# A hybrid decoder layer on one core: negated row maxima, whole copies of the softmax outputs, and low parts and a state decay moved from VectorE to GpSimd

## The reference, cut to what matters

```
h = rms_norm(x, norm1_w);  y = h @ w_in                      # 1024 -> 3852 columns
fox:       logits = q @ k.T * 64**-0.5 + c_i - c_j (causal), p = softmax(logits), o = p @ v        # 4 heads of 64
retention: o = chunked linear attention with fixed decay; o = head_rms(o) * silu(rg)               # 4 heads of 64
gdn:       per chunk: u = u0 - w @ state;  o = q_g @ state + attn @ u                              # 4 heads of 128
           state = state * exp(g_last) + k_tail.T @ u
           o = head_rms(o) * gdn_norm_w * silu(gz)
x = x + concat(fox, retention, gdn) @ w_out                  # 1024 -> 1024
h = rms_norm(x, norm2_w)
x = x + sum over the two chosen experts of (silu(h @ w1) * (h @ w3) * gate) @ w2     # 32 experts, width 256
out = rms_norm(x, final_norm_w)
```

## Time and profile before

| | us |
|---|---|
| median of 3 runs (620.01 to 622.05) | 621.25 |
| the profiled execution's own time | 619.92 |
| its span, first to last instruction | 618.0 |
| busy: PE | 579.1 (94%) |
| busy: DVE | 245.6 (40%) |
| busy: ACT | 198.6 (32%) |
| busy: POOL | 179.8 (29%) |
| mean granted TensorE clock | 0.995 |

### The profile page before, as it was taken

The page is one execution under the profiler, slowest core; times in us unless marked ns, Lnnn a source line. Parts: engine busy times, 40 slices in busy tenths (PEclk is TensorE's granted clock), DMA queues, the critical chain, the costliest instruction groups (busy, mean ns, idle before and its releaser), DMA issues.

```text
span 618.0 us, 12011 instructions
## 1 busy us (share of the span) xinstructions
PE 579.1 (94%) x4922; PEld 446.4 (72%) x4922; DVE 245.6 (40%) x618; ACT 198.6 (32%) x429; POOL 179.8 (29%) x118
## 2 busy tenths in 40 slices
PE   7999999999999999999899999999999999987892
PEld 5987887799999888856679998666555565654440
DVE  6135553592216711287732146323332233321117
ACT  7344544523324261634635321111111121111113
POOL 1443434173268422421433301111112111120014
PEclk9999999999999999999999999999999999999997
DMA  9665443422121122003788878999999999999975
GB/s 338 202 187 157 146 134 97 134 70 51 56 70 36 37 69 70 1 2 122 271 325 305 318 265 313 357 421 423 428 422 427 423 429 423 423 425 428 419 299 229
DMA packets 44857, 150.63 MB, mean 244 GB/s; under 512 B 8552, under 2 KB 29760, under 8 KB 38274
## 3 DMA queue, kind: packets, MB, share of 16 engines
q1 hardware_dynamic: 40208, 141.67, 60.4%
q0 software_dynamic: 4528, 8.15, 3.6%
q10 hardware_dynamic: 66, 0.03, 0.0%
HBM read 141.69 MB, written 16.27 MB: 256 GB/s over the span
## 4 chain that ended last, share of the span: by engine, by line
PE 62%; DMA 19%; DVE 11%; issue 4%; ACT 2%; POOL 1%; SPq 0%; DVEq 0%; POOLq 0%; ACTq 0%
PE bank L772 29%; PE bank L796 9%; DMA xg<-h2d,tok 8%; DMA w<-in_expert_w_dram 8%; PE bank L1184 5%; PE bank L1138 4%; PE bank L1160 3%; PE bank L1084 2%; PE bank L1098 2%; DMA yd<-oy,dst 2%; DMA yt<-yd 1%; DVE Dm L1801 1%; PE bank L1078 1%; PE bank L1054 1%; DMA raw<-in_w_in_dram 1%
## 5 line engine op out<-in xcount | busy, mean ns | idle before, releaser
L1506 POOL TENSOR_TENSOR wlo<-raw,whi 128x1024 fp32r<-128x1024 f32 (+1 forms) x25 | 59.9, 2400 | 95.7 <-ACT whi L1207 95.7
L772 PE MATMUL bank<-wlo,hHi 128*128 128x256 f32 (+2 forms) x224 | 64.9, 290 | 0.0
L1138 PE MATMUL bank<-w,xT 128*64 128x256 f32 x512 | 58.2, 380 | 5.1 <-issue 5.1
L772 PE MATMUL bank<-whi,hHi 128*128 128x256 f32 (+1 forms) x208 | 59.9, 288 | 3.2 <-DVE cacc L1701 1.4
L1611 POOL DMA_INDIRECT yd<-oy,dst x15 | 15.1, 1009 | 162.7 <-DVE oy L2140 162.7
L1160 PE MATMUL bank<-w,xT 128*64 128x256 f32 x512 | 58.2, 380 | 2.6 <-DMA w<-in_expert_w_dram 2.6
L1184 PE MATMUL bank<-w,hidT 128*64 128x512 f32 x256 | 58.5, 599 | 1.1 <-ACT hidT L1483 1.1
L1138 PEld LDWEIGHTS bank<-w,xT 128*64 128x64 f32 x512 | 37.8, 137 | 29.4 <-issue 14.5
L772 PE MATMUL bank<-whi,hLo 128*128 128x256 f32 (+1 forms) x208 | 58.7, 282 | 0.0
L1160 PEld LDWEIGHTS bank<-w,xT 128*64 128x64 f32 x512 | 36.4, 137 | 21.5 <-DMA w<-in_expert_w_dram 3.5
L2123 DVE SCALAR_TENSOR_TENSOR hid<-bank,slot,sa 128x256 f32<-128x256 f32 x16 | 10.8, 676 | 94.6 <-issue 92.1
(11 more groups left out here) (374 smaller groups left out, 1121.2 us busy)
## 6 DMA issues: line engine op xcount, KB each, us to landing
w<-in_expert_w_dram SPq DMA_DIRECT2D x44, 2048.0 KB, 21.5
raw<-in_w_in_dram SPq DMA_DIRECT2D x24, 512.0 KB, 3.9
w<-in_expert_w_dram SPq DMA_DIRECT2D x8, 1024.0 KB, 7.1
yd<-zt SPq DMA_DIRECT2D x8, 512.0 KB, 5.1
yt<-yd SPq DMA_DIRECT2D x4, 1024.0 KB, 9.0
raw<-in_w_in_dram SPq DMA_DIRECT2D x6, 520.0 KB, 7.2
X<-in_x_dram SPq DMA_DIRECT2D x4, 512.0 KB, 5.8
raw<-in_w_out_dram SPq DMA_DIRECT2D x4, 512.0 KB, 3.3
```

Source lines behind the costliest of these rows:

```text
L772: m = pe.matmul(o, l, r, start=(at == 0 and c == 0 and i == 0), stop=(at == parts - 1 and kc == chunks[-1] and i == 2), skip_group_check=True)
L1138: m = pe.matmul(pb[3][r, 0:FF], xT[:, c, r], w1[u % 4][:, e, c * FF:(c + 1) * FF], start=(c == 0), stop=(c == KC - 1), skip_group_check=True)
L1506: pool.tensor_tensor(low_of(g), raw_of(g), high_of(g).bitcast(F32), ALU.subtract).then_inc(wlo_done, 1)
```

## The change

- **Negated maxima.** The scores' reduction now scales by -1/8 and takes a minimum, so that it writes `nmx` directly, and `Sx` is the negated, scaled score; ACT's exponential takes scale -1. The 16 instructions of line 1886 are gone. ACT waits for the release of the scores' bank in place of `sx_ready`.
- **Whole copies.** ACT writes each fox output twice: `hHi` as before, and `foxF` in full precision, and this second copy frees the bank. POOL forms `hLo` = foxF - hHi (8 instructions); DVE's 8 of line 1948 are gone. PE's four tiles wait for POOL's count `foxl_done`.
- **State decay.** POOL multiplies the state by its decay into `Stg` (k = 2 and 4); DVE's four instructions per step become one addition, bank + Stg.
- **Order on POOL.** Its list becomes a loop over k; the eight low parts stand between the older instructions, and the product with the retention gate stands behind all of them.
- **Order on DVE.** The low parts of chunks 4 and 5 stand ahead of the wait for the retention gate and of `retention_step`.

```diff
@@ -346,6 +346,8 @@
         Sx = [[at(f"Sx{i}{j}", [P, S], FX[j + 2 * i]) for j in range(2)] for i in range(2)]
         Pf = [[at(f"Pf{i}{j}", [P, S], FX[6 + j + 2 * i]) for j in range(2)] for i in range(2)]
         PT = [[at(f"PT{i}{j}", [P, T, P], FX[(4 if i == 0 else 10) + j]) for j in range(2)] for i in range(2)]
+        foxF = at("foxF", [P, NFOX, P], R1 + 4 * KB)
+        Stg = at("Stg", [P, NH, P], R1 + 13 * KB)
         small = at("small", [P, 1024], R9 + 16 * KB)
         attnT = at("attnT", [P, T, NH, P], R5)
         def pair(name, slot):
@@ -414,7 +416,7 @@
         uinit = sem("uinit")
         y_copied = sem("y_copied")
         rot_done = sem("rot_done")
-        sx_ready = sem("sx_ready"); pe_ready = sem("pe_ready"); pf_ready = sem("pf_ready"); foxh_done = sem("foxh_done"); gsq_read = sem("gsq_read"); scores_read = sem("scores_read")
+        pe_ready = sem("pe_ready"); pf_ready = sem("pf_ready"); foxl_done = sem("foxl_done"); stg_ready = sem("stg_ready"); gsq_read = sem("gsq_read"); scores_read = sem("scores_read")
         zg_done = sem("zg_done"); sqr_done = sem("sqr_done"); ssr_done = sem("ssr_done"); rtr_done = sem("rtr_done")
         mixr_done = sem("mixr_done"); mixg_done = sem("mixg_done"); rk_done = sem("rk_done"); silu2_done = sem("silu2_done"); s_x2 = sem("s_x2in")
         s_out = sem("s_out")
@@ -977,7 +979,7 @@
                 at = TILES.index(b)
                 if 1 <= at <= 2:
                     step(NFOX - 1 + at)
-                wait_read(pe, ("fO", T + at))
+                pe.wait_ge(foxl_done, T + at + 1)
 
             def turn_mixed(q):
                 for c in QUARTERS[q]:
@@ -1381,10 +1383,10 @@
                     w = (t + 1) * P
                     for i in range(2):
                         u = 2 * k + i
-                        act.wait_ge(sx_ready, u + 1)
+                        wait_read(act, ("fS", k, i))
                         if k >= 2:
                             wait_full(act, ("fT", k - 2, i))
-                        act.activation(Pf[k % 2][i][:, 0:w], Sx[k % 2][i][:, 0:w], ACT.Exp, scale=HD ** -0.5,
+                        act.activation(Pf[k % 2][i][:, 0:w], Sx[k % 2][i][:, 0:w], ACT.Exp, scale=-1.0,
                                        bias=nmx[:, u:u + 1], accum_out=rs[:, u:u + 1]).then_inc(pe_ready, 1)
                 if k in OO:
                     n = OO[k]
@@ -1422,11 +1424,14 @@
                     pr, t = FOX[k - 2]
                     name = ("fO", k - 2)
                     wait_full(act, name)
-                    act.activation(hHi[:, pr, t * P:(t + 1) * P], psum(name)[:, 0:P], ACT.Copy).then_inc(foxh_done, 1)
+                    act.activation(hHi[:, pr, t * P:(t + 1) * P], psum(name)[:, 0:P], ACT.Copy)
+                    release(act.activation(foxF[:, k - 2, :], psum(name)[:, 0:P], ACT.Copy), name)
             for q, chunks in enumerate(QUARTERS[1:]):
                 for c in chunks:
                     name = ("mT", c)
                     wait_full(act, name)
+                    if c == 2:
+                        act.wait_ge(foxl_done, NFOX)
                     act.activation(hHi[:, c, :], psum(name)[:, :], ACT.Copy).then_inc(hhi_done, 1)
                 weight_high(act, GR_IN + 2 + q)
             weight_high(act, GR_IN + 5)
@@ -1570,18 +1575,35 @@
                 m4 = mix[:, t, GW:D].rearrange("p (h n) -> p h n", h=NH)
                 pool.tensor_tensor(m4, m4, kbg[:, t, :, :], ALU.mult).then_inc(og_done, 1)
 
-            for t in range(T):
-                wait_read(pool, ("o", t))
-                pool.tensor_tensor(gsq[t][:, :, :], kbg[:, t, :, :], kbg[:, t, :, :], ALU.mult).then_inc(sqr_done, 1)
-                if t == 0:
-                    pool.wait_ge(zg_done, 1)
-                if t < T - 1:
-                    by_heads(t)
-            for pr in range(NH // 2):
-                wait_read(pool, ("rB", pr))
-            pool.tensor_tensor(osq[:, :, :], oret[:, :, :], oret[:, :, :], ALU.mult).then_inc(sqr_done, 1)
-            pool.wait_ge(pf_ready, 2 * NFOX)
-            by_heads(T - 1)
+            def decayed_state(n):
+                wait_read(pool, ("Sp", n - 1))
+                decay = egl[:, 4 * n:4 * n + 4].unsqueeze(2).broadcast_to([P, NH, P])
+                pool.tensor_tensor(Stg[:, :, :], St[:, :, :], decay, ALU.mult).then_inc(stg_ready, 1)
+
+            for k in range(KSTEPS):
+                if k in OO:
+                    t = OO[k]
+                    if 1 <= t < T - 1:
+                        decayed_state(t)
+                    wait_read(pool, ("o", t))
+                    pool.tensor_tensor(gsq[t][:, :, :], kbg[:, t, :, :], kbg[:, t, :, :], ALU.mult).then_inc(sqr_done, 1)
+                    if t == 0:
+                        pool.wait_ge(zg_done, 1)
+                    if t < T - 1:
+                        by_heads(t)
+                if k == max(RT):
+                    for pr in range(NH // 2):
+                        wait_read(pool, ("rB", pr))
+                    pool.tensor_tensor(osq[:, :, :], oret[:, :, :], oret[:, :, :], ALU.mult).then_inc(sqr_done, 1)
+                if k >= 2:
+                    pr, t = FOX[k - 2]
+                    tk = slice(t * P, (t + 1) * P)
+                    wait_read(pool, ("fO", k - 2))
+                    pool.tensor_tensor(hLo[:, pr, tk], foxF[:, k - 2, :], hHi[:, pr, tk].bitcast(F32),
+                                       ALU.subtract).then_inc(foxl_done, 1)
+                if k == NFOX - 1:
+                    pool.wait_ge(pf_ready, 2 * NFOX)
+                    by_heads(T - 1)
             pool.tensor_tensor(mix[:, :, 256:GW], mix[:, :, 256:GW], oret[:, :, :], ALU.mult).then_inc(or_done, 1)
 
             for g in range(GR_IN, GR - 2):
@@ -1879,11 +1901,9 @@
                         if k >= 2:
                             dve.wait_ge(pe_ready, u - 3)
                         j = dve.tensor_tensor_reduce(out=Sx[k % 2][i][:, 0:w], in0=psum(name)[:, 0:w], in1=cB8[:, 2 * pr + i, 0:w],
-                                                     scale=1.0, scalar=-3.0e38, op0=ALU.add, op1=ALU.max,
-                                                     accum_out=mx[:, u:u + 1])
+                                                     scale=-float(HD ** -0.5), scalar=3.0e38, op0=ALU.add, op1=ALU.min,
+                                                     accum_out=nmx[:, u:u + 1])
                         release(j, name)
-                        dve.wait_ge(free[BANK[name][0]], BANK[name][1] + 1)
-                        dve.tensor_scalar(nmx[:, u:u + 1], mx[:, u:u + 1], -float(HD ** -0.5), None, ALU.mult).then_inc(sx_ready, 1)
                 if k in WS and k > min(WS):
                     state_sum(WS[k])
                 if k in OO and OO[k] < T - 1:
@@ -1893,11 +1913,8 @@
                     if n == 0:
                         j = dve.tensor_copy(St[:, :, :], v4(name))
                     else:
-                        for h in range(NH):
-                            j = dve.scalar_tensor_tensor(out=St[:, h, :], in0=St[:, h, :],
-                                                         scalar=egl[:, 4 * n + h:4 * n + h + 1],
-                                                         in1=psum(name)[:, h * P:(h + 1) * P],
-                                                         op0=ALU.mult, op1=ALU.add)
+                        dve.wait_ge(stg_ready, n)
+                        j = dve.tensor_tensor(St[:, :, :], v4(name), Stg[:, :, :], ALU.add)
                     release(j, name)
                 if k in RS:
                     n0, j0 = RS[k]
@@ -1940,12 +1957,6 @@
                     link(dve.tensor_tensor(rn, rn, rqs[:, :], ALU.mult))
                     dve.wait_ge(og_done, T)
                     gate_step(0)
-                if k >= 2:
-                    pr, t = FOX[k - 2]
-                    name = ("fO", k - 2)
-                    dve.wait_ge(foxh_done, k - 1)
-                    tk = slice(t * P, (t + 1) * P)
-                    release(dve.tensor_tensor(hLo[:, pr, tk], psum(name)[:, 0:P], hHi[:, pr, tk].bitcast(F32), ALU.subtract), name)
 
             def retention_step():
                 m = mix[:, :, 256:GW].rearrange("p t (h n) -> p t h n", h=NH)
@@ -1962,9 +1973,11 @@
             dve.sem_inc(slots_freed, 1)
             dve.wait_ge(rtr_done, 2)
             link(dve.reciprocal(ssx4, ssx4))
+            for c in MT[:2]:
+                low_part(c)
             dve.wait_ge(or_done, 1)
             retention_step()
-            for c in MT:
+            for c in MT[2:]:
                 low_part(c)
             dve.tensor_copy(rankb[:, :], const("rankm"))
             dve.tensor_copy(onesb[:, :], ones)
```

## The result

The changed kernel takes 617.4 us (median, 617.1 to 617.57) against 621.21 for the kernel before beside it; the ratio is 0.9942, 95% interval 0.9926 to 0.9958. Both intervals allow 0.9944 to 0.9958, a gain of 2.6 to 3.5 us. The profiled execution took 617.34 us with a span of 615.2.

A forecast was written before the change was run, and what follows sets the result against it. PE's waits on DVE and ACT between 260 and 314 us were taken to move the end one for one. Seven terms (+0.15, -0.3, -0.43, -0.15, +0.27, -1.0, -0.3) summed to -1.76 us: 619.5 us, range 617.9 to 621.7.

The forecast's parts named there:

- the waits of PE that I named: Six PE waits between 260 and 314 us, 4.75 us in all, for banks or tiles DVE or ACT has not read.
- the maxima: Multiplications gone from DVE: -0.3 us at PE's wait for step 3's vb (278.99) and -0.15 at 299.47.
- Behind tile 2: PE's 0.90 us wait at 313.66 for the low parts of chunks 4 and 5: -0.3 us (+0.3 to -0.6).
- fO(6): PE's 0.99 us wait at 305.42 for fO(5)'s bank goes whole, as ACT frees it: -1.0 us (0.8 to 1.1).
- the division: Step 0's division on DVE at 265.63 meets POOL's first Stg product, delaying vb: +0.15 us (0 to 0.25).
- fS(7): PE's 0.88 us wait at 299.47 for a bank ACT frees after two exponentials: -0.15 us (0 to -0.25).
- State decay: PE's 0.68 us wait at 286.42 for Sp(2)'s bank: four DVE instructions become one addition, -0.43 us.
- Tile 0: New PE wait at 302.01, start of the w_out product, for POOL's low part of fO(4): +0.27 us (0 to +0.5).
- GpSimd as the bound: Rival, chance 0.17: POOL replaces DVE, small low parts cost 0.8 us, tiles 0 and 2 wait; 620.4 us.
- holding the ports over several instructions: Rival, chance 0.08: GpSimd keeps ports over back-to-back instructions, delaying step 6's last division and the second gate scaling; 623.2 us.
- The stream hiding the gain: Rival, chance 0.05: the expert weight stream hides the gain; 621.2 us.
- No new wait: Rival, chance 0.15: POOL gets through before PE each time, the last wait shrinks fully; -2.6, 618.6 us.

The follow-up runs named there:

- one_max: The kernel before with the negated maxima alone; 619.82 us, ratio 0.9985 to the kernel before.
- all_but_max: The changed kernel with the maxima as before (16 multiplications back on DVE); 618.45 us, ratio 0.9964 to the kernel before.
- one_state: The kernel before with the state's decay on GpSimd alone; 620.33 us, ratio 0.9993 to the kernel before.
- one_fox: The kernel before with the whole copies and the low parts of the fox outputs on GpSimd alone; 623.75 us, ratio 1.0049 to the kernel before.
- held_back: The changed kernel with 26 more transposes on PE ahead of mT(4), written over by those that follow; 620.21 us, ratio 0.9983 to the kernel before.
- again: The changed kernel once more, unaltered, measured beside the later runs; 618.5 us, ratio 0.9957 to the kernel before.

## Why the prediction was right or wrong

The direction and the mechanism held: the gain came from the waits of PE that I named, it was passed on as far as the loads of the results, and GpSimd did not become the bound. The size did not. The forecast was 619.5 us and the range ended at 617.9; the first measurement was 617.4, the second, 618.5, lies inside the range. The sum of -1.76 should have been -2.83. Of the missing 1.07 us the maxima are 0.49 (0.94 against 0.45), what is listed under "Behind tile 2" 0.21, fO(6) 0.20 and the division 0.15. The last microsecond of the 3.8 belongs to no term. In the two profiles 0.98 us was gained behind h2d, which is within what that part varies by itself, and the medians scatter by as much; what makes it is open. The terms' own bounds add up to -2.70 and -0.42; the -0.35 of the sum was a slip.

- **Negated maxima: the step that failed.** I priced a multiplication by the distance from its start to the next reduction, 0.12 us, and named the wait ahead of it only as a little more (0.12 to 0.16 each). The runs show 0.23 each: `one_max` and `all_but_max` give 1.27 us alone and 0.94 within the change, against 0.45. At fS(7) I let ACT's first exponential come 0.2 us earlier and the second be held by it. The first came 0.18 earlier, as forecast, but the second had stood 0.85 us behind it, the distance of the two reductions, and now stands 0.72 behind: with what follows, 0.34 in place of 0.15. What to read was the distance between the two reductions, 0.85, against the distance at which DVE starts the next instruction behind a 512-column one that nothing interrupts: 0.61, from 278.15 to 278.76.
- **The division beside GpSimd's product** cost 0, not 0.15: the product took 1.03 us, below both ends of my 1.10 to 1.27.
- **State decay** -0.43: `one_state` says 0.42.
- **Tile 0** +0.27: measured +0.18. The duration was right. With the maxima as before the step was the forecast one (+0.27 in `all_but_max`, +0.26 in `one_fox`); without the multiplications `gsq`, ahead of `osq` on GpSimd, took 1.18 us in place of 1.26 and let the low part start that much sooner.
- **fO(6)** -1.0: measured -1.20. The wait of 0.99 went whole; the six transposes ahead of it also went from 0.94 to 0.82 us. Before, they started at 303.50, while the last division still ran (303.28 + 0.42); probably they waited for it, which no run tests by itself.
- **Behind tile 2** -0.3: measured -0.51; the scalings and GpSimd's last low part alternated as I had described, some 0.9 us earlier than forecast, as PE was.
- **The rivals.** GpSimd as the bound, or holding the ports over several instructions: refuted by GpSimd's rows, the low part of 0.45 us and the one of 0.75 between the two scalings. The stream hiding the gain: refuted by `held_back` up to the loads of the results. "No new wait" at -2.6 was nearest in size, for another reason than the one I gave it.
- **What I did not see** is how the parts depend on each other. I wrote that the retention's product would end near 312.5 and called it hidden. It is hidden only because the low parts were moved; without that, it costs 4.6 us. I had costed that edit at 0.3. A fall of the granted clock behind a long wait was in no term and no rival either.

The spread of medians was also too small in my range: in four comparisons the kernel before came out at 620.36, 620.73, 620.97 and 621.21 us, the changed one at 617.4 and 618.5.

## What to carry to other kernels

Price a small instruction that waits for its own engine by the distance between its neighbours with it and without it, not by its own duration: here 0.23 us against 0.02 to 0.06 for one that waits for nothing. When work is moved to another engine, look for what is queued behind it there and who waits for that; a reordering that seems worth half a microsecond may be what makes the move pay. And where medians differ by a microsecond for no reason, count positions from an instruction ahead of the change.

## What the runs showed of the hardware that I had not expected

- A wait of 3.42 us on PE was followed by a granted clock of 0.57 to 0.59 over four microseconds, in both runs that had it, and cost a further 1.44 and 1.60 us. In the changed kernel and the one before, whose waits there are all under 1 us, the clock is 1.00 from 300 to 334 us (the rows and those after the change).
- The start of the program has two outcomes, whatever the kernel. The first product of the projection, behind a wait of 1.0 to 1.4 us, took either 0.39 or 0.58 us. Rows of the kernel before and of the changed kernel, the first and the fourth product:

```profile
11.78 0.39 PE L772 MATMUL bank<-whi,hHi 128*128 128x260 f32 x1 [1.07 <-POOL wlo L1506]
...
12.25 0.28 PE L772 MATMUL bank<-whi,hHi 128*128 128x260 f32 x1
```

```profile
11.87 0.59 PE L774 MATMUL bank<-whi,hHi 128*128 128x260 f32 x1 [1.15 <-POOL wlo L1511]
...
12.68 0.42 PE L774 MATMUL bank<-whi,hHi 128*128 128x260 f32 x1
```

It is not the first product alone: the products behind it stand 0.12 us apart in the one case and 0.22 in the other, for 12 products, and the eight transposes that follow take 1.03 or 1.38 to 1.84 us. That is what half the clock would do, but the granted clock of these microseconds reads 1.00 in both. In the five profiles with 0.39 the first score product stands at 259.55 to 259.81 us, in the nine with 0.58 or 0.59 at 260.48 to 261.14. The length of the wait does not sort them (1.37 with 0.39, 1.01 with 0.58). That microsecond is in the time of every profiled execution here, and it was against the changed kernel in its two profiles and for the kernel before in its one. What decides it was not tried, and whether it makes the two groups of times under `again` is not shown.
